# Turning the own rows, the sample rows and the sample's residual rows in one group of transposes, and copying rows through DRAM

## The reference: what is computed

```
xn = rmsnorm(h, norm_ffn_g)                 # 256 + 32 tokens
eidx, g = 128 chosen experts of each token, with their gates
act = gelu(einsum('nd,ned->ne', xn, u[eidx])) * g
h = h + einsum('ne,ned->nd', act, v[eidx])
y = rmsnorm(h, norm_final_g)
```

## Time and profile before

| | |
|---|---|
| median of 3 executions | 2010.14 us (2008.37 to 2010.9) |
| the profiled execution's own time | 2011.87 us, of which its span is 2010.0 us |
| TensorE busy | 98% of the span |
| VectorE, ScalarE, GpSimd busy | 76%, 43%, 35% |
| DMA | 531.27 MB, mean 264 GB/s |
| granted TensorE clock | 1.00 in all stretches read here |

### The profile page before, as it was taken

One profiled execution on the slowest core, in us unless ns is written; L12 is line 12 of the kernel. 1 busy time (PEld: TensorE's weight loads), 2 busy tenths in 40 slices (PEclk: granted clock), 3 DMA queues, 4 the chain that ended last, 5 costly groups with the idle time before them and its releaser, 6 DMA issues.

```text
span 2010.0 us, 29296 instructions
## 1 busy us (share of the span) xinstructions
PE 1969.0 (98%) x11128; PEld 1753.3 (87%) x11128; DVE 1526.5 (76%) x2291; ACT 863.6 (43%) x873; POOL 709.3 (35%) x488
## 2 busy tenths in 40 slices
PE   6999998999999999999999999999999999999998
PEld 6987776999999999999999999988888888888886
DVE  5988755455788898898889998577677767777786
ACT  4340136334544555445454555533343333344343
POOL 2010110220336687888868783010100101213310
PEclk9999998899999999999999999999999999999999
DMA  5464294444444778878887897889989899998984
GB/s 211 167 193 142 86 392 168 145 165 139 145 143 146 249 251 293 293 274 281 279 300 270 305 339 283 319 311 361 339 328 340 324 348 345 353 367 342 375 313 147
DMA packets 101226, 531.27 MB, mean 264 GB/s; under 512 B 19376, under 2 KB 21568, under 8 KB 45792
## 3 DMA queue, kind: packets, MB, share of 16 engines
q1 hardware_dynamic: 71552, 408.93, 56.8%
q0 software_dynamic: 24304, 106.45, 14.6%
q10 hardware_dynamic: 5296, 14.98, 2.0%
HBM read 491.34 MB, written 38.14 MB: 263 GB/s over the span
## 4 chain that ended last, share of the span: by engine, by line
PE 89%; DVE 5%; DMA 2%; ACT 2%; issue 1%; POOL 0%; DVEq 0%; SPq 0%; ACTq 0%; POOLq 0%
PE acc L1592 18%; PE mis L1939 17%; PE acc L1939 17%; PE acc L1593 9%; PE acc L1569 5%; PE acc L1571 5%; PE acc L1570 5%; PE acc L1618 5%; PE acc L1712 3%; DVE wl L917 1%; DMA raw<-in_u 1%; PE mis L1687 1%; ACT wh L540 1%; PE mis L1663 1%; DVE xhl L925 0%
## 5 line engine op out<-in xcount | busy, mean ns | idle before, releaser
L917 DVE TENSOR_TENSOR wl<-raw,wh 128x2048 fp32r<-128x2048 f32 x310 | 711.1, 2295 | 283.4 <-ACT wh L540 270.7
L540 ACT ACTIVATE wh<-raw 128x2048 fp32r<-128x2048 f32 x310 | 593.2, 1915 | 564.3 <-DMA raw<-in_v 409.3
L1592 PE MATMUL acc<-xhl,wh 128*128 128x448 f32 x2048 | 643.5, 375 | 1.4 <-DVE wl L917 1.2
L1593 PE MATMUL acc<-xhl,wl 128*128 128x224 f32 x2048 | 540.5, 264 | 0.0
L1592 PEld LDWEIGHTS acc<-xhl,wh 128*128 128x128 f32 x2048 | 384.2, 188 | 32.5 <-DVE wl L917 2.9
L1593 PEld LDWEIGHTS acc<-xhl,wl 128*128 128x128 f32 x2048 | 390.8, 191 | 0.0
L2094 POOL DMA_INDIRECT G<-gsum,cell x224 | 353.6, 1579 | 82.6 <-issue 69.8
L1569 PE MATMUL acc<-xhl,wh 128*128 128x288 f32 x768 | 230.4, 300 | 15.2 <-DVE wl L953 14.3
L1570 PE MATMUL acc<-xhl,wh 128*128 128x288 f32 x768 | 227.3, 296 | 0.0
L1571 PE MATMUL acc<-xhl,wl 128*128 128x288 f32 x768 | 226.9, 295 | 0.0
L1569 PEld LDWEIGHTS acc<-xhl,wh 128*128 128x128 f32 x768 | 145.4, 189 | 18.2 <-DVE wl L953 14.3
(11 more groups left out here) (323 smaller groups left out, 2585.3 us busy)
## 6 DMA issues: line engine op xcount, KB each, us to landing
raw<-in_u SPq DMA_DIRECT2D x128, 1024.0 KB
raw<-in_v SPq DMA_DIRECT2D x128, 1024.0 KB
raw<-in_w_mix SPq DMA_DIRECT2D x28, 1024.0 KB
G<-zero SPq DMA_DIRECT2D x16, 1024.0 KB, 14.0
raw<-in_w_out SPq DMA_DIRECT2D x16, 1024.0 KB
raw<-in_w_pq SPq DMA_DIRECT2D x16, 1024.0 KB
gin<-G SPq DMA_DIRECT2D x32, 512.0 KB
h<-hbg ACTq DMA_DIRECT2D x32, 448.0 KB
```

The lines of the kernel that those rows point to most:

```text
L540: act.activation(wh[:, n % 4], raw[:, n % 4], ACT.Copy).then_inc(hi_done, 1)
L917: dve.tensor_tensor(wl[:, n % 4], raw[:, n % 4], wh[:, n % 4].bitcast(F32), ALU.subtract).then_inc(lo_done, 1)
L1592: pe.matmul(acc[:, s, 0:2 * NU], wh[:, s, j, :], xu[:, j, 0:2 * NU], start=(j == 0), stop=False)
L1593: ins = pe.matmul(acc[:, s, 0:NU], wl[:, s, j, :], xuh[:, j, :], start=False, stop=(j == DT - 1))
```

## The change

The three groups of transposes become one, after u tile 2. `xs4` now holds four different or equal blocks of 32 columns: the own rows, the normalized sample rows, the residual rows, and the own rows again. ACT takes the group out into `xrow_a` in steps 3 and 4, two banks each. In step 5 ACT issues two copies of 32 rows (256 KB each) to DRAM: the sample rows to the new tensor `sample_rows` and the residual rows to `hst_rows`. In step 6 ACT waits for both copies to land, and then issues two copies that write the own rows over these two blocks. Later SP fills `xrow` with four DMAs of 256 KB, each to 32 partitions, at its steps 121 to 124. The groups after u tiles 117 and 121, their evacuations and the copy of `xs` four times over are gone, and TensorE's u tiles 4 to 123 are one loop.

```diff
-XROW_IT, HST_IT, TURN_S = 29, 30, 1
-XROW_EVAC, HST_EVAC = 4 * XROW_IT + TURN_S + 1, 4 * HST_IT + TURN_S + 1
+ROW_EVACS, ROW_COPIES, ROW_REPEATS = {3: (0, 1), 4: (2, 3)}, 5, 6
...
+                if n == 121:
+                    sp.wait_ge(dot_a_done, PICKS_A)
+                    sp.wait_ge(xr_out, 16)
+                if 121 <= n < 121 + P // NS:
+                    q = n - 121
+                    sp.dma_start(xrow[NS * q:NS * q + NS, :], dr["xr"]).then_inc(xrow_in, 16)
...
+            def row_copies():
+
+                act.wait_ge(xrow_out, 4)
+                act.dma_start(dr["xr"], xrow_a[NS:2 * NS, :]).then_inc(xr_out, 16)
+                act.dma_start(dr["hst"], xrow_a[2 * NS:3 * NS, :]).then_inc(hst_out, 16)
+
+            def row_repeats():
+
+                act.wait_ge(xr_out, 16)
+                act.wait_ge(hst_out, 16)
+                for q in (1, 2):
+                    act.dma_start(xrow_a[NS * q:NS * q + NS, :], xrow_a[0:NS, :]).then_inc(xrow_a_in, 16)
+
+            def rows_together():
+
+                act.wait_ge(xs_ready, 1)
+                for q in (0, 3):
+                    act.activation(xs4[:, :, q, :], xs[:], ACT.Copy).then_inc(xs4_ready, 1)
+                act.activation(xs4[:, :, 2, :], hT[:, :, NP_:N], ACT.Copy).then_inc(xs4_ready, 1)
...
             def sample_rows():
 
-                dve.wait_ge(xrow_turned, 1)
-                own.done(dve.tensor_tensor(xs[:], hT[:, :, NP_:N], bcast(par[:, Q_GFFN:Q_GFFN + DT], NS, 2), ALU.mult))
+                dve.wait_ge(xs_ready, 1)
+                at = xs4[:, :, 1, :]
+                own.done(dve.tensor_tensor(at, hT[:, :, NP_:N], bcast(par[:, Q_GFFN:Q_GFFN + DT], NS, 2), ALU.mult))
                 own.wait(0)
-                dve.tensor_tensor(xs[:], xs[:], bcast(rstd[:, 1, NP_:N], DT, 1), ALU.mult).then_inc(xs_ready, 1)
+                dve.tensor_tensor(at, at, bcast(rstd[:, 1, NP_:N], DT, 1), ALU.mult).then_inc(xs4_ready, 1)
...
                 if n == 0:
                     own_x()
+                    sample_rows()
...
-                if n == 4 * XROW_IT - 2:
-                    sample_rows()
...
-            for s in range(4):
-                u_slot(XROW_IT, s)
-                if s == TURN_S:
-                    pe.wait_ge(xrow_out, 4)
-                    pe.wait_ge(xs4_ready, 2)
-                    turn_rows()
-            for s in range(4):
-                u_slot(HST_IT, s)
-                if s == TURN_S:
-                    pe.wait_ge(xrow_out, 8)
-                    for c in range(DT):
-                        ins = pe.transpose(mis[0:NS, c // 4, P * (c % 4):P * (c % 4) + P], hT[:, c, NP_:N], ident)
-                    ins.then_inc(hst_turned, 1)
-            for s in range(4):
                 u_slot(31, s)
```

More of the change, by code:

```diff
@@ L305, in build @@
                 xs4 = sb(o, "xs4", [P, DT, P // NS, NS])
-            with ExitStack() as o:
-                hst = sb(o, "hst", [P, D])
         ring_a = (ring_a0, ring_a1, ring_a2)
@@ L368, in build @@
         dot_done, sgelu_done, sact_ready, vsum_done = sem("dot_done"), sem("sgelu_done"), sem("sact_ready"), sem("vsum_done")
-        hst_turned, hst_copied, hst_out, hst_in = sem("hst_turned"), sem("hst_copied"), sem("hst_out"), sem("hst_in")
+        xrow_in, xrow_a_in, hst_out, hst_in = sem("xrow_in"), sem("xrow_a_in"), sem("hst_out"), sem("hst_in")
+        xr_out = sem("xr_out")
         res_turned, part_in, part_sum = sem("res_turned"), sem("part_in"), sem("part_sum")
@@ L809, in _, with row_evac @@
             act.sem_inc(gelu_done, 1)
-            def row_evac(to, c, count):
+            def row_evac(c):
                 if c == 0:
[L814 to L825, removed]
+                    act.wait_ge(xrow_turned, 1)
+                act.activation(xrow_a[:, 512 * c:512 * c + 512], mis[:, c, :], ACT.Copy).then_inc(xrow_out, 1)
+            def row_copies():
[12 more added lines that the diff above has]
+                act.activation(xs4[:, :, 2, :], hT[:, :, NP_:N], ACT.Copy).then_inc(xs4_ready, 1)
             def gelu_a(c):
@@ L843, in u_hook @@
                 if n == 1:
[L844 to L856, removed]
+                    rows_together()
+                for c in ROW_EVACS.get(n, ()):
+                    row_evac(c)
+                if n == ROW_COPIES:
+                    row_copies()
+                if n == ROW_REPEATS:
+                    row_repeats()
                 if n == 4 * 31 + 2:
@@ L1387, in own_dot @@
                     dve.wait_ge(xrow_out, 4)
+                    dve.wait_ge(xrow_a_in, 32)
                 dve.wait_ge(pick_a_in[own_ring(g)], 16 * len(ring_users(g)))
@@ L1394, in pick_dot @@
                 if g == 0:
-                    dve.wait_ge(xrow_out, 8)
+                    dve.wait_ge(xrow_in, 16 * (P // NS))
                 dve.wait_ge(pick_in[g % 2], 16 * (g // 2 + 1))
@@ L1883, in _ @@
                     pe.wait_ge(pq_out, 16)
-                    pe.wait_ge(xs4_ready, 1)
+                    pe.wait_ge(xs4_ready, 4)
                     turn_rows()
-            with pe.Fori(1, XROW_IT) as i:
+            with pe.Fori(1, 31) as i:
                 for s in range(4):
@@ L1889, in _ @@
             for s in range(4):
-                u_slot(XROW_IT, s)
-                if s == TURN_S:
-                    pe.wait_ge(xrow_out, 4)
-                    pe.wait_ge(xs4_ready, 2)
-                    turn_rows()
-            for s in range(4):
-                u_slot(HST_IT, s)
-                if s == TURN_S:
-                    pe.wait_ge(xrow_out, 8)
-                    for c in range(DT):
-                        ins = pe.transpose(mis[0:NS, c // 4, P * (c % 4):P * (c % 4) + P], hT[:, c, NP_:N], ident)
-                    ins.then_inc(hst_turned, 1)
-            for s in range(4):
                 u_slot(31, s)
             def residual():
-                pe.wait_ge(hst_copied, 4)
+                pe.wait_ge(xrow_out, 4)
                 for t in (1, 0):
@@ L2219 @@
     dr["ha"] = nc.dram_tensor("h_own", (P, NKEYS, NA), F32, kind="Internal").ap()
+    dr["xr"] = nc.dram_tensor("sample_rows", (NS, D), F32, kind="Internal").ap()
     dr["hst"] = nc.dram_tensor("hst_rows", (NS, D), F32, kind="Internal").ap()
```

## The result

The changed kernel takes 2014.34 us (median of 13 runs, 2012.4 to 2019.43) against 2009.65 us for the kernel before (median of 13, 2007.64 to 2012.48). The ratio is 1.0023, 95% interval [1.0015, 1.0032]: slower by 4.7 us, where 2009.7 us with a gain of 0.45 us was forecast.

What follows compares the result with a forecast made beforehand. TensorE was taken to bound the kernel from u tile 3 to the end. Saving, early and late costs: -3.85 + 1.2 + 2.2 = -0.45 us, from the median 2010.14 to 2009.7 us; range 2006.3 to 2012.8.

Steps and rivals of the forecast that it cites:

- The saving: TensorE loses two transpose groups, 3.46 us, and the stall ahead of u tile 117, 0.39 us: at most 3.85 us gained.
- The early place: U tiles 8 to 12: copies and ACT's wait delay tile 9's `wh` by 1.35 us, stalling TensorE 1.2 us.
- `wh` of tile 9 held behind its load and behind ACT's issues: Early: copies slow tile 9's load, and ACT's step 6 wait plus two issues delay its `wh`; taken as 1.35 us.
- The held case: Slower rival, chance 0.12: ACT waits in step 6 for copies landing after 9.8 us; TensorE stalls 4.7 us, total 2013.2 us.
- the upper end of the early cost: U tiles 8 to 12: stall of 2.5 us if ACT's issues come behind the late load (1.5 + 0.9, less 0.15).
- The late place: U tiles 122 to 125: tile 123's load comes late and late copies delay loads, costing 2.2 us.
- it is late by 0.88 us before any DMA is added: U tile 123: without the group it is wanted 1.73 us sooner, against 0.85 us of slack.
- I take 1.1: Late place: one 256 KB copy to 32 partitions ahead of tile 123's load costs 1.1 us; 0.6 at full rate.
- I add 0.2: Late place: the copies ahead of tiles 124 and 125 add 0.2 us, the stall giving their loads more time.
- The upper end of 4.2 us: Late place: 0.9 + 3 x 1.1 us if all three copies push the loads.
- the slower one: Rival at the early place, chance 0.12: ACT held in step 6 by late landing copies, +3.1 us, 2013.2 us.
- copies to 32 partitions go at half the rate of full traffic: Sign expected in the changed trace, for the copies to 32 partitions: 1.10 us each for 0.6 at 427 GB/s.

Runs made afterwards that it cites:

- e_bare: Changed kernel without its early and late copies, except the residual rows' copy to DRAM in step 124; constant for sample rows: 2004.42 us against 2009.86, ratio 0.9975.
- e_none: Changed kernel without the four late copies to `xrow`, which VectorE fills with a constant in step 121: 2007.17 us against 2010.18 for the kernel before.
- e_norep: Changed kernel without the two repeats of the own rows and the sample rows' multiplications; all four blocks are own rows: ratio 1.0021 to the kernel before.
- e_gather: Changed kernel with POOL's gathers of the picked rows starting only when tile 124 has been used, late copies kept: ratio 1.0014 to the kernel before.
- e_wide: e_src with each late copy writing 512 columns of all 128 partitions, same bytes: ratio 1.0002 to the kernel before.
- e_src: Changed kernel with each late copy reading its own 256 KB piece of DRAM, three DRAM-to-DRAM copies added in steps 30, 34, 38: ratio 1.0031.
- e_one: Changed kernel with only the first late copy; DVE writes a constant into the other 96 rows: tiles 115 to 127 late by 4.60 us, ratio 0.0018 above e_none.
- e_rep8: Changed kernel with the two repeats of the own rows in ACT's step 8 instead of 6: tile 10 late by 0.59 us, late place by 8.49.
- e_move: Changed kernel with the four late copies three steps later, at SP's steps 124 to 127: ratio 1.0016 to the kernel before.

## Why the prediction was wrong, point by point

**The saving, 3.85 us: right.** Tiles 115 to 127 take 3.89 us less without copies (64.05 less 60.16). There is one group of 16 transposes on `xs` left in the u stage, and the stall ahead of tile 117 is gone. As a time, e_bare gains 5.0 us, interval 2.8 to 7.0; in the profiled runs its u stage is 3.5 us shorter than before.

**The early place, 1.2 us: the size about right, the step wrong.** Tiles 3 to 20 take 0.80 us more than before, and 1.25 more in e_none than in e_bare. But it is not `wh` of tile 9 held behind its load and behind ACT's issues. The rows answer to the earlier trace rows; ACT, then TensorE at tile 10:

```profile
676.10 0.35 ACTq L824 DMA_DIRECT2D sample_rows<-xrow_a  x1
676.48 0.59 ACTq L825 DMA_DIRECT2D hst_rows<-xrow_a  x1
...
684.03 2.21 ACTq L832 DMA_DIRECT2D xrow_a<-xrow_a  x2
686.29 1.92 ACT L544 ACTIVATE wh<-raw 128x2048 fp32r<-128x2048 f32 x1 [2.05 <-DMA raw<-in_u]
...
694.51 1.92 ACT L544 ACTIVATE wh<-raw 128x2048 fp32r<-128x2048 f32 x1 [5.72 <-DMA raw<-in_u]
...
698.95 0.47 PE L1601 MATMUL acc<-xhl,wh 128*128 128x448 f32 x1 [0.71 <-DVE wl L925]
```

Counted from u tile 0, which starts 4.87 us earlier in this execution, `wh` of tile 9 is 0.8 us later than before, without harm; `wh` of tile 10 waits 5.72 us for its load, and that tile starts late. The held case, which I gave 0.12, did not come: ACT issued the repeats at 684.03 and still had to wait 2.05 us for tile 9's load. The 9.8 us on which that case was built are the landing of POOL's load of these rows back into SBUF, not of a copy to DRAM; that one took the 3.5 us. And the upper end of the early cost, given as 2.5, comes to 2.25 by its own terms. Which of the early copies makes tile 10 late is open: with none it is on time (e_bare), without the repeats it is still late (e_norep), and the run without the copies to DRAM but with the repeats was not made, since the repeats wait for them. The stretch also differs by itself, from 85.52 (e_gather) to 89.12 us (e_wide), in kernels that are alike up to step 30, so single traces of it show little.

**The late place, 2.2 us: the step that failed.** It measured 8.29 us (68.45 less 60.16). By its terms:

- "it is late by 0.88 us before any DMA is added": 0.00. In e_none the load is issued at 1257.0 and its `wh` starts at 1267.1, 10.1 us later, where before it took 11.5. I had held the load's landing fixed in time while TensorE moved; it moved too.
- "I take 1.1" for a copy, and "I add 0.2" for those behind it: with the 0.6 us of its bytes a copy took 1.6 to 2.3 us of all engines' time, part of it in the packets of others (four such copies in e_src and in the changed kernel, less e_none). I had priced a copy by the time its own queue's packets took. The upper end of 4.2 us was built from this same price.
- What was missing is the sum over the window. I asked what one copy adds ahead of one load. But the copies are issued at 1244.42, 1249.29, 1253.82 and 1258.83, the gathers take 6.8 us of all engines from about 1255 on, and the load of tile 123, issued at 1253.44, is under way until 1270. Its lead is used up by all of it together; in the traces the runs with only one of the two in that window are late by 0.00 and 0.63 us.
- The clock: tile 123 took 1.7 us more than the usual 5.01, with a granted clock of 0.50 from 1272 to 1276, behind the stand of 6.05 us. The prediction had no term for it.

So the sum is -3.89 + 0.80 + 8.29 + 0.23 = +5.43 us in the profiled runs, +4.7 us in the medians, and -0.45 was forecast. Of the rivals none had this: the slower one lay at the early place. That copies to 32 partitions go at half the rate of full traffic was my estimate from one read of 32 partitions, 1.10 against 0.6 us. For writes no run shows it by itself: e_src and e_wide, late by 6.17 and 2.66 us, differ in the source too, and two reads of 32 partitions in e_norep took 0.6 us each.

What stays open: the copies' price with no gathers near, whether it is the 32 partitions or the single piece of DRAM that makes them dear, the early copy at fault, and what the longer executions of e_gather hold.

## What to carry to other kernels

Before adding DMAs to a stretch, add up all traffic there as time of all engines (share times length), at the rate that it will really get (9.42 MB in 32.0 us here, where e_none moved 11.40 MB in 29.7), and compare it with the lead of the loads; a price per copy ahead of one load says little when the engines are full. A transfer can be charged to its neighbours as well, as the gathers' packets here with 0.418 us for 0.328: look at the packets of the other queues. Here copies into 128 partitions from a spread source were the cheap form (late by 2.66 us), and copies into 128 partitions that read 32 rows four times were not (11.39). When an experiment leaves work out, look at what stands in its place: a constant written by VectorE made a tile late by 2.33 us in e_one. A saving on the bounding engine of 3.9 us was real, and 256 KB copies "beside" it took it back twice.

## What the runs showed of the hardware

Full DMA engines can be slow ones: 1.02 of the share at 260 GB/s against 414 GB/s twelve microseconds later in the same kernel. The packets of gates beside copies into 32 partitions took 0.22 to 0.30 us for 0.159. SP's queue went in the order of issue in the kernel before: the packets of the load issued at 1254.42 start from 1255.37 to 1258.53, those of the `hin` issued at 1254.79 from 1258.47 to 1260.40. Two copies out of 32 partitions to DRAM went at the full rate in e_norep (0.309 us a packet), the same two in e_rep8 did not (0.434). In the run with wide copies whose source is read four times, two issues on SP took 3.41 and 4.93 us that otherwise take 0.33 and 0.61, and the 128 packets of the first copy took 3.9 us for 1.7. And after TensorE stood 6.05 us the granted clock was 0.50, where stands of about 1 us (1.0 in e_none) left it at 1.00 from 690 to 705. Between these the runs differ: it was 1.00 from 1276 to 1284 behind the stand of 2.4 us in e_wide, and 0.62 from 1302 to 1306 behind that of 2.0 us in e_move.
